# Placing the expert weights with three bf16 products per token instead of one f32 product

## The reference, cut to what matters

```python
def one_block(xb):
    q = (xb @ w_q).reshape(tb, PEER_HEADS, 2, PEER_KEY_DIM)
    sc = jnp.einsum('thpk,hpnk->thpn', q, sub_keys)
    s1, i1 = lax.top_k(sc[:, :, 0], PEER_TOPK)
    s2, i2 = lax.top_k(sc[:, :, 1], PEER_TOPK)
    ...
    top_s, pos = lax.top_k(cand, PEER_TOPK)
    idx = jnp.take_along_axis(cidx, pos, axis=-1)       # i1 * 128 + i2
    gw = jax.nn.softmax(top_s, axis=-1)
    act = jax.nn.gelu(jnp.einsum('td,thkd->thk', xb, u[idx]))
    return jnp.einsum('thk,thkd->td', act * gw, v[idx])
```

## Time and profile before

| | |
|---|---|
| median of 3 runs | 2109.36 us |
| the profiled execution's own time | 2112.14 us |
| its span | 2110.0 us |
| TensorE matmul busy | 2021.6 us (96%) |
| TensorE weight load busy | 1856.2 us (88%) |
| VectorE (DVE) busy | 1258.7 us (60%) |
| ScalarE (ACT) busy | 973.1 us (46%) |
| GpSimd (POOL) busy | 1283.8 us (61%) |
| granted TensorE clock, mean | 0.984 |

### The profile page before, as it was taken

One profiled execution on the slowest core, in us unless ns is written; L12 is line 12 of the kernel. 1 busy time (PEld: TensorE's weight loads), 2 busy tenths in 40 slices (PEclk: granted clock), 3 DMA queues, 4 the chain that ended last, 5 costly groups with the idle time before them and its releaser, 6 DMA issues.

```text
span 2110.0 us, 40295 instructions
## 1 busy us (share of the span) xinstructions
PE 2021.6 (96%) x13604; PEld 1856.2 (88%) x13604; DVE 1258.7 (60%) x2835; ACT 973.1 (46%) x1431; POOL 1283.8 (61%) x624
## 2 busy tenths in 40 slices
PE   7988999999999999999989879999999999999998
PEld 7787999999999888888787869999999998888886
DVE  6555099538888544444475550994388885444444
ACT  4444454653333454554544434446533334445454
POOL 5334679976666555555463337899766665555553
PEclk9999999999999999999999999999999999999999
DMA  6423455554444555555534225545444445555554
GB/s 208 145 80 100 160 185 167 171 175 140 139 139 139 169 190 196 190 195 193 184 121 151 90 81 174 195 159 175 166 140 140 138 140 176 194 194 191 196 190 139
DMA packets 93242, 338.44 MB, mean 160 GB/s; under 512 B 10353, under 2 KB 10737, under 8 KB 93169
## 3 DMA queue, kind: packets, MB, share of 16 engines
q1 hardware_dynamic: 93168, 337.53, 47.7%
HBM read 336.44 MB, written 1.05 MB: 160 GB/s over the span
## 4 chain that ended last, share of the span: by engine, by line
PE 85%; DVE 7%; POOL 3%; issue 2%; ACT 1%; DMA 1%; POOLq 0%; DVEq 0%; SPq 0%; ACTq 0%
PE PS L885 33%; PE PS L829 10%; PE PS L824 10%; PE PS L825 10%; PE PS L837 5%; PE PS L530 4%; POOL WL L444 3%; DVE G L1382 2%; PE PS L514 2%; PE PS L515 2%; PE PS L750 2%; PE PS L519 2%; PE PS L496 1%; PE PS L625 1%; DVE G L1379 1%
## 5 line engine op out<-in xcount | busy, mean ns | idle before, releaser
L444 POOL TENSOR_TENSOR WL<-ring,WH 128x1024 fp32r<-128x1024 f32 x360 | 910.0, 2533 | 486.1 <-ACT WH L955 244.6
L1119 ACT CAST WH<-ring 128x1024 fp32r<-128x1024 f32 x512 | 538.0, 1051 | 814.1 <-PE PS L825 380.8
L470 POOL TENSOR_TENSOR HL<-G,HH 128x256 fp32r<-128x256 f32 x256 | 372.5, 1455 | 324.4 <-ACT HH L1212 324.3
L1702 DVE TENSOR_TENSOR WL<-ring,WH 128x1024 fp32r<-128x1024 f32 x248 | 303.7, 1225 | 371.0 <-ACT WH L1119 371.0
L824 PE MATMUL PS<-HH,WH 128*128 128x256 f32 x2048 | 512.2, 288 | 0.0
L825 PE MATMUL PS<-HL,WH 128*128 128x256 f32 x2048 | 501.3, 283 | 0.0
L825 PEld LDWEIGHTS PS<-HL,WH 128*128 128x128 f32 x2048 | 392.2, 192 | 0.0
L824 PEld LDWEIGHTS PS<-HH,WH 128*128 128x128 f32 x2048 | 391.8, 191 | 0.0
L885 PE MATMUL PS<-WH,HH 128*128 128x512 f32 x1024 | 315.4, 389 | 3.0 <-issue 3.0
L885 PE MATMUL PS<-WH,HL 128*128 128x512 f32 x1024 | 315.3, 389 | 0.0
L829 PE MATMUL PS<-HH,WL 128*128 128x256 f32 x2048 | 289.1, 284 | 12.4 <-POOL WL L444 12.4
(11 more groups left out here) (237 smaller groups left out, 2306.8 us busy)
## 6 DMA issues: line engine op xcount, KB each, us to landing
ring<-stream SPq DMA_DIRECT2D x636, 512.0 KB, 3.3
X<-x_t SPq DMA_DIRECT2D x4, 256.0 KB, 4.4
out_t<-X SPq DMA_DIRECT2D x2, 512.0 KB, 2.7
CN<-consts SPq DMA_DIRECT2D x1, 843.5 KB, 9.7
WF<-last SPq DMA_DIRECT2D x1, 512.0 KB, 10.2
PR<-params SPq DMA_DIRECT2D x2, 239.0 KB, 4.4
CN<-consts SPq DMA_DIRECT2D x1, 64.0 KB, 5.1
```

The source lines that it names most:

```text
L444: nc.gpsimd.tensor_tensor(WL[:, b, :], ring[:, slot, :], WH[:, b, :].bitcast(F32), ALU.subtract).then_inc(done, 1)
L470: nc.gpsimd.tensor_tensor(GL[:, s, :], G[:, tile, :], GH[:, s, :].bitcast(F32), ALU.subtract).then_inc(L.gl_ready, 1)
L1119: nc.scalar.copy(WH[:, b, :], ring[:, slot, :]).then_inc(L.hi_ready, 1)
L1702: V.tensor_tensor(WL[:, s % 2, :], ring[:, (U0 + s) % SLOTS, :], WH[:, s % 2, :].bitcast(F32), ALU.subtract).then_inc(L.vlo_ready, 1)
```

## The change

The one-hot matrices become bf16. `O2` keeps its form (3 rows of 43). The weight of each pair is split into three bf16 parts whose sum is the f32 weight; the parts are kept as f32 values in PSUM banks 2 and 3, and `O1` becomes 3 x 128 wide, one row for each part, made by one `scalar_tensor_tensor` whose second input is read from PSUM. `place` then does three bf16 products per token, accumulated in PSUM. The copy of the later tiles' weights moves from DVE's `weigh` to a new function `keep` on ScalarE, which is called after each `WH` cast; TensorE's wait for `w_used` now waits for ScalarE, and `keep` waits for a new semaphore `w_mul` of DVE. Six DVE instructions in each layer make the parts in place of one copy.

```diff
-        OH = sb("OH", [P, 8, 2 * OW])
-        IOB = sb("IOB", [P, 3 * IW], BF16)
+        WB = sb("WB", [P, 2, TT, P], BF16)
+        OH = sb("OH", [P, 8, OW + 3 * P], BF16)
+        IOB = sb("IOB", [P, 3 * IW + P], BF16)
...
+        w_whole = PS[:, 2:4, 3 * P:4 * P]
+        w_part = [PS[:, 2:4, a * P:(a + 1) * P] for a in range(3)]
...
                             o = bank[6 + g][:, i * P:(i + 1) * P]
-                            mm = nc.tensor.matmul(o, O2[:, 4 * g + i, 0:P], O1[:, 4 * g + i, 0:P],
-                                                  start=True, stop=True)
+                            for a in range(3):
+                                mm = nc.tensor.matmul(o, O2[:, 4 * g + i, 0:P], O1[:, 4 * g + i, a * P:(a + 1) * P],
+                                                      start=(a == 0), stop=(a == 2))
...
+                    def keep(g):
+                        n = direct_tiles(g)
+                        w = bank[6 + g % 2].rearrange("p (i e) -> p e i", i=4)
+                        act.wait_ge(L.w_mul, g + 1)
+                        nc.scalar.copy(G[:, n:TILES, 4 * g:4 * g + 4], w[:, n:TILES, :]).then_inc(L.w_used, 1)
...
-                            high_k(HK + 2 * q + 2)
-                            high_k(HK + 2 * q + 3)
+                            for e in range(2):
+                                high_k(HK + 2 * q + 2 + e)
+                                keep(2 * q + e)
                             gelu_pair(q)
...
+                    keep(GROUPS - 2)
                     high_v0(0)
+                    keep(GROUPS - 1)
...
-                    V.tensor_copy(slotW, bank[2][:, 0:SEQ]).then_inc(L.rt_free, 1)
+                    step(V.tensor_copy(WB[:, 0, :, :], w_whole))
+                    V.tensor_copy(w_part[0], WB[:, 0, :, :])
+                    step(V.tensor_tensor(w_part[2], w_whole, WB[:, 0, :, :], ALU.subtract))
+                    step(V.tensor_copy(WB[:, 1, :, :], w_part[2]))
+                    V.tensor_copy(w_part[1], WB[:, 1, :, :])
+                    V.tensor_tensor(w_part[2], w_part[2], WB[:, 1, :, :], ALU.subtract).then_inc(L.rt_free, 1)
...
-                            ins = V.tensor_scalar(O1[:, slot, 0:3 * IC].rearrange("p (a b) -> p a b", a=3),
-                                                  iota3[:, :, 0:IC], slotT[:, 0, t:t + 1], slotW[:, t:t + 1],
-                                                  ALU.is_equal, ALU.mult)
+                            parts = PS[:, 2 + t // P, 0:3 * P].rearrange("p (a n) -> p a n", a=3)[:, :, t % P]
+                            ins = V.scalar_tensor_tensor(out=O1[:, slot, :].rearrange("p (a n) -> p a n", a=3),
+                                                         in0=bc(iota1, 1, 3), scalar=slotT[:, 0, t:t + 1],
+                                                         in1=bc(parts, 2, P), op0=ALU.is_equal, op1=ALU.mult)
...
                         acts = G[:, 0:n, 4 * g:4 * g + 4]
-                        V.tensor_tensor(acts, acts, w[:, 0:n, :], ALU.mult)
-                        V.tensor_copy(G[:, n:TILES, 4 * g:4 * g + 4], w[:, n:TILES, :]).then_inc(L.w_used, 1)
+                        V.tensor_tensor(acts, acts, w[:, 0:n, :], ALU.mult).then_inc(L.w_mul, 1)
```

More of the change, by code:

```diff
@@ L66 @@
 GROUPS = SEQ // 4
-OW, IC, IW = 130, 43, 44
+OW, IC, IW = 132, 43, 44
 TILES = EXPERTS // P
@@ L158, in first_direct, with direct_tiles @@
     return min(GROUPS, 2 * q + 4)
+def direct_tiles(g):
+    return HK + 2 * sum(first_direct(q) <= g for q in range(HK // 2))
 class Signals:
@@ L220, in __init__ @@
         self.w_used = sem("w_used")
+        self.w_mul = sem("w_mul")
         self.pair_done = sem("pair_done")
@@ L280, in program @@
         slotT = sb("slotT", [P, 2, SEQ])
-        slotW = sb("slotW", [P, SEQ])[:, :]
-        OH = sb("OH", [P, 8, 2 * OW])
-        IOB = sb("IOB", [P, 3 * IW], BF16)
+        WB = sb("WB", [P, 2, TT, P], BF16)
+        OH = sb("OH", [P, 8, OW + 3 * P], BF16)
+        IOB = sb("IOB", [P, 3 * IW + P], BF16)
         STG = sb("STG", [P, 2, 2, SEQ])
@@ L373, in program @@
         RT = late(12544, 768).rearrange("p (t k n) -> p t k n", t=TT, k=3)
-        O1 = OH[:, :, 0:OW]
-        O2 = OH[:, :, OW:2 * OW]
-        iota3 = IOB[:, :].rearrange("p (a b) -> p a b", a=3)
+        O2 = OH[:, :, 0:OW]
+        O1 = OH[:, :, OW:OW + 3 * P]
+        iota3 = IOB[:, 0:3 * IW].rearrange("p (a b) -> p a b", a=3)
+        iota1 = IOB[:, 3 * IW:3 * IW + P]
+        w_whole = PS[:, 2:4, 3 * P:4 * P]
+        w_part = [PS[:, 2:4, a * P:(a + 1) * P] for a in range(3)]
         GH, GL = HH, HL
@@ L856, in _ @@
                         for t in range(TT):
-                            mm = nc.tensor.transpose(bank[k][:, t * P:(t + 1) * P], RT[:, t, k, :], ident)
+                            o = bank[k][:, t * P:(t + 1) * P] if k < 2 else w_whole[:, t, :]
+                            mm = nc.tensor.transpose(o, RT[:, t, k, :], ident)
                         mm.then_inc(L.rt_tr, 1)
@@ L1371, in _ @@
                         dve.wait_ge(cn_in, 16)
-                        step(nc.vector.tensor_copy(iota3[:, :, 0:IC], cn("iota").rearrange("p (a b) -> p a b", a=3)))
+                        nc.vector.tensor_copy(iota3[:, :, 0:IC], cn("iota").rearrange("p (a b) -> p a b", a=3))
+                        step(nc.vector.tensor_copy(iota1, cn("iota", 0, P)))
                     dve.wait_ge(L.padded, 1)
@@ L1649, in one_hot @@
                                             slotT[:, 1, t:t + 1], None, ALU.is_equal)
-                            ins = V.tensor_scalar(O1[:, slot, 0:3 * IC].rearrange("p (a b) -> p a b", a=3),
-                                                  iota3[:, :, 0:IC], slotT[:, 0, t:t + 1], slotW[:, t:t + 1],
-                                                  ALU.is_equal, ALU.mult)
+                            parts = PS[:, 2 + t // P, 0:3 * P].rearrange("p (a n) -> p a n", a=3)[:, :, t % P]
+                            ins = V.scalar_tensor_tensor(out=O1[:, slot, :].rearrange("p (a n) -> p a n", a=3),
+                                                         in0=bc(iota1, 1, 3), scalar=slotT[:, 0, t:t + 1],
+                                                         in1=bc(parts, 2, P), op0=ALU.is_equal, op1=ALU.mult)
                         ins.then_inc(L.o_ready, 1)
                     def weigh(g):
-                        n = HK + 2 * sum(first_direct(q) <= g for q in range(HK // 2))
+                        n = direct_tiles(g)
                         w = bank[6 + g % 2].rearrange("p (i e) -> p e i", i=4)
```

## The result

The changed kernel takes 2091.89 us, the median of 4 runs (2090.62 to 2094.45), against 2109.41 us before (the median of 4 runs, one more than the 2109.36 us above has). The ratio is 0.9917, with a 95% interval of 0.9902 to 0.9932: 17.5 us or 0.8% faster. The forecast was 2096 us. A second measurement of the same kernel, on another chip, gave 0.9913 (0.9884 to 0.9942).

A forecast was written before the change was run, and what follows sets the result against it. TensorE was taken as the bound, DVE second. TensorE's gain of 14.5 us, less 0.6 for DVE and 0.4 for the rest, made 13.5 us, so 2109.4 became 2096 us; range 2083 to 2127, the forecast's own 2090 to 2102.

The forecast's parts named there:

- The bound and the price of placing: TensorE bounds the placing stage; placing one group costs 0.88 us, over 128 groups 113 us, none of it hidden.
- The price of a bf16 product: Each of twelve placing products on TensorE takes 0.060 us, within bounds of 0.057 and 0.11 us.
- cheap load of L857: Transposes' weight loads on TensorE take 140 ns, about one clock a column, taken as a sign that bf16 loads are cheap.
- Rival A: On TensorE the bf16 load isn't hidden or not cheap: slower, 2127 us at 81 ns a product; chance 0.22.
- The uncovered f32 load: On TensorE, the last bf16 product doesn't cover the tile's first f32 load: 0.05 us more a tile.
- The sum for a tile: TensorE's tile with placing: 2.88 + 0.77 = 3.65 us instead of 3.763, 14.5 us gained over 128 groups.
- Sum of four pairs: DVE's one-hots for a group: four times O2 at 0.19 plus O1 at 0.525 us, 2.86 us.
- pass TensorE at group 53: DVE's period exceeds TensorE's 3.65 us from group 53; the last nine groups lose 0.6 us in both layers.
- Rival B: DVE becomes the bound because O2 stays at 0.255 us: 2107 us, near 2135 with O1 at 0.60 too; chance 0.18.
- Rival C: On TensorE, a product at 0.057 us and no uncovered load: tile 3.56 us, time 2087 us; chance 0.13.
- its cover: On ACT, a cast delayed 0.4 us by the copy is hidden by later work's slack; without cover, 38 us lost.
- The size: Whole kernel: 14.5 - 0.6 - 0.4 = 13.5 us less, giving 2096 us.

The follow-up runs named there:

- the interleaved kernel: Changed kernel with each token's three bf16 products put ahead of another pair of f32 products, four changes of kind in a tile instead of one: 2117.86 us.
- the two kernels whose one-hots wait for GpSimd: Changed kernel with the weight parts read from SBUF instead of PSUM, 2308.77 us; changed kernel with O2 made as one row of 128, 2276.71 us.

## Why the prediction was right, point by point

- **The bound and the price of placing** (0.883 us a group, nothing hidden): right. Moving the copy alone changed nothing, and the products taken away came back in full until DVE held it.
- **The price of a bf16 product**: forecast 0.060 us within 0.057 to 0.11, measured 0.057. The argument from the cheap load of L857 and the spacing of L662 held, and Rival A does not occur. By the forecast's own way of reading listed durations (about 83 ns fixed, 192 - 128 x 0.85), a load at one clock a column would be listed with about 136 ns; 98 ns were measured, so the load is cheaper still, which the time can't show, since it is hidden either way. The Trainium skill, "TensorE: Matmul & The Clock Gate", section "Back-to-back issue gap", gives about 81 ns per product for a sustained stream of load and product pairs at 128 columns. This stream has 57 ns, and the measurement decides.
- **The uncovered f32 load**: forecast 0.05 us, 0.05 in the sum of the tile (0.737 - 12 x 0.057) and 0.064 in the interleaved kernel. Right. It had been an inference from two durations; the interleaving turned it into a measured cost. That the cost is the load's is argued from the rows of the timeline.
- **The sum for a tile**: forecast 3.65 us, measured 3.617. The term that was too large is the product's, 12 x 3 ns, so 4.6 us of the time (4.2 by the rounded sums of the tile).
- **DVE**: O2 forecast at 0.19 us, measured 0.19. O1 at 0.525, measured 0.52 (602 ns long; 613 forecast). Sum of four pairs 2.86, measured 2.86. DVE was said to pass TensorE at group 53 and to lose 0.6 us; with 3.617 us it should have passed it earlier still, yet TensorE shows no wait. The double buffer of one-hots took all of that, where I had given it only a part. This is argued from the absence of a wait and not tested by itself.
- **Rival B** (DVE as the bound) did not occur, but it was near: the run with f32 numbers for O2 is this rival, 12 us slower than the changed kernel, where the prediction has 11 us between this rival and the forecast (2107 and 2096 us).
- **Rival C** came true in one of its two terms: the product costs its 0.057 us, but the uncovered load is there. So 2091.89 us lies about halfway between the forecast and C's 2087 us, near the lower end of the forecast's own 2090 to 2102.
- **ACT**: right that its cover holds. What the text did not foresee is that ACT now waits 41.9 us for pair products, and why. The pair product has two SBUF inputs, and one of them met GpSimd's subtraction:

```profile
583.30 2.39 POOL L455 TENSOR_TENSOR WL<-ring,WH 128x1024 fp32r<-128x1024 f32 x1 [1.23 <-ACT WH L1132]
583.41 2.56 DVE L1704 TENSOR_TENSOR G<-G,STG 128x256 f32<-128x256 f32 x1
```

In the kernel before, the one of the same width took 0.42 us: it started at 589.18 us, 0.20 us before GpSimd's next subtraction, and here it starts 0.11 us after one. DVE waited for TensorE in all 64 groups then, which would keep the two in step; that the lost wait is what moved them together is argued, not shown. The trace has one such long instance in each layer (2.56 and 2.58 us). From 583 us on DVE is behind by this much and has no gap in which to catch up (busy for all 37 us from 583 to 620 and all 30 from 620 to 650); the buffer between it and TensorE hides it. The prediction has no such term, so that it cost nothing is luck.

- **The size**: forecast 13.5 us, measured 17.5. The placing alone gave 18.7 us, where the forecast had 14.5 less 0.6 for DVE. The forecast also took 0.4 us off for the end of the stage, which no run shows by itself. The 1.2 us between 18.7 and 17.5 are within the interval of about 3 us either way.

The versions that beat both kernels all drop products, and with them parts of the weight: 2070.15 us with one product, 2063.42 and 2065.84 with two parts, and 2034.61 with one part. With all three parts, none of the versions beats the changed kernel.

## What to carry to other kernels

Where many small products run between larger ones, price them by start-to-start times, and count the changes from bf16 to f32: a bf16 product is too short to cover the next f32 load, so keep the bf16 ones together. When a change trades TensorE time for DVE time, write DVE's period out group by group, since a gain stops where the other engine's period begins. And beside a busy GpSimd keep DVE instructions away from the forms that wait for it: one operand in PSUM cost nothing here (602 against 606 ns), and a source and destination that differ in form (3 rows of 43 into one run of 129) cost 32 ns an instruction; giving up either cost about 200 us.

## What the runs showed that I had not expected

For the two kernels whose one-hots wait for GpSimd I had put the loss at 110 us or more and 20 us or more, and it was over 200 and about 185. The blocking comes on top of a DVE with hardly any slack. With the parts in SBUF the stretch from the first placing of layer 0 to the last grew from 227.86 to 335.61 us, by 108 us, and in layer 1 from 228.03 to 336.51 us, which together is the whole loss. In layer 0 TensorE was idle for 335.61 - 261.07 = 75 us of it, and its busy time grew by 33 us at a granted clock that is partly at the lower level. Whether the lower clock cost any time is not shown: DVE's own instruction took as long as in the changed kernel (606 against 602 ns), and DVE was busy for 333 us of the 336, so it alone could set this pace.
